# Sine product of the indexer queries behind the first head's shift, query root ahead of the keys' squares, value transposition one chunk later

## The reference

```python
(fq, fk, fv, ff, dq, dk, dv, iq, ik, iw, mq, g) = jnp.split(u @ w_in[l], SPLIT_POINTS, axis=-1)
fq = rmsnorm(fq.reshape(B, S, FOX_HEADS, FOX_HEAD_DIM), fox_q_norm[l])
fk = rmsnorm(fk.reshape(B, S, FOX_HEADS, FOX_HEAD_DIM), fox_k_norm[l])
o_a = fox_attention(fq, fk, fv, logf)
...
iq = rope(iq.reshape(B, S, IDX_HEADS, IDX_DIM), cos_i, sin_i)
...
km, vm = jnp.split(rmsnorm(mem, mem_norm[l]) @ w_mem_kv[l], 2, axis=-1)
km = rmsnorm(km.reshape(B, M, MEM_HEADS, MEM_HEAD_DIM), mem_k_norm[l])
mq = rmsnorm(mq.reshape(B, S, MEM_HEADS, MEM_HEAD_DIM), mem_q_norm[l])
o_c = memory_attention(mq, km, vm)
```

## Time and profile before

| | us |
|---|---|
| three runs, median | 2227.75 |
| lowest and highest of them | 2225.24, 2231.1 |
| the profiled execution | 2225.2 |
| its span | 2223.1 |
| TensorE busy | 2016.6 (91% of the span) |
| VectorE, GpSimd, ScalarE busy | 1099.5, 1223.2, 505.8 |
| mean granted TensorE clock | 0.962 |

### The profile page before, as it was taken

The page is one execution under the profiler, slowest core; times in us unless marked ns, Lnnn a source line. Parts: engine busy times, 40 slices in busy tenths (PEclk is TensorE's granted clock), DMA queues, the critical chain, the costliest instruction groups (busy, mean ns, idle before and its releaser), DMA issues.

```text
span 2223.1 us, 25286 instructions
## 1 busy us (share of the span) xinstructions
PE 2016.6 (91%) x8955; PEld 1627.6 (73%) x8955; DVE 1099.5 (49%) x1308; ACT 505.8 (23%) x916; POOL 1223.2 (55%) x752
## 2 busy tenths in 40 slices
PE   7999999788877789988999999998898869999996
PEld 6888887467656677777778888885677648888884
DVE  5333520556555558765664333009878685333104
ACT  3111100333333333243121111002266421111001
POOL 4666666245534445634666666654454456666661
PEclk9999999899999999999999999999999979999998
DMA  4333323212211113201233333233200012333220
GB/s 146 95 94 97 101 95 85 69 57 72 62 39 38 39 49 84 86 11 38 87 94 95 97 101 95 95 94 85 67 1 1 20 57 86 100 97 94 95 94 38
DMA packets 259808, 163.83 MB, mean 74 GB/s; under 512 B 30380, under 2 KB 249582, under 8 KB 259614
## 3 DMA queue, kind: packets, MB, share of 16 engines
q1 hardware_dynamic: 258080, 157.90, 24.2%
q10 hardware_dynamic: 1662, 5.06, 0.7%
HBM read 160.81 MB, written 2.13 MB: 73 GB/s over the span
## 4 chain that ended last, share of the span: by engine, by line
PE 74%; DVE 17%; ACT 4%; issue 3%; POOL 2%; ACTq 0%; DMA 0%; POOLq 0%; DVEq 0%; SPq 0%
PE bank L710 12%; PE bank L711 12%; PE bank L712 12%; PE bank L779 5%; PE bank L777 5%; PE bank L778 5%; PE bank L971 3%; DVE work L1910 3%; PE bank L973 3%; PE bank L972 3%; DVE work L1971 2%; PE bank L841 2%; PE bank L1176 1%; PE bank L1177 1%; PE bank L1178 1%
## 5 line engine op out<-in xcount | busy, mean ns | idle before, releaser
L597 POOL TENSOR_TENSOR w_lo<-raw,w_hi 128x1024 fp32r<-128x1024 f32 x298 | 744.5, 2498 | 24.9
L595 POOL TENSOR_SCALAR w_hi<-raw 128x1024 fp32r<-128x1024 f32 x298 | 319.4, 1072 | 735.3 <-PE bank L712 344.4
L710 PE MATMUL bank<-u_hi,w_hi 128*128 128x512 f32 x1184 | 476.7, 403 | 27.9 <-DVE u_lo L1859 18.4
L711 PE MATMUL bank<-u_lo,w_hi 128*128 128x512 f32 x1184 | 465.5, 393 | 0.0
L712 PE MATMUL bank<-u_hi,w_lo 128*128 128x512 f32 x1184 | 465.2, 393 | 0.0
L710 PEld LDWEIGHTS bank<-u_hi,w_hi 128*128 128x128 f32 x1184 | 224.7, 190 | 90.7 <-issue 25.5
L711 PEld LDWEIGHTS bank<-u_lo,w_hi 128*128 128x128 f32 x1184 | 225.3, 190 | 49.7 <-issue 4.8
L712 PEld LDWEIGHTS bank<-u_hi,w_lo 128*128 128x128 f32 x1184 | 225.0, 190 | 47.9
L777 PE MATMUL bank<-hid_hi,w_hi 128*128 (+1 forms) x480 | 186.7, 389 | 0.0
L778 PE MATMUL bank<-hid_lo,w_hi 128*128 (+1 forms) x480 | 186.7, 389 | 0.0
L779 PE MATMUL bank<-hid_hi,w_lo 128*128 (+1 forms) x480 | 186.7, 389 | 0.0
(11 more groups left out here) (462 smaller groups left out, 3304.2 us busy)
## 6 DMA issues: line engine op xcount, KB each, us to landing
raw<-in_w_in SPq DMA_DIRECT2D x52, 512.0 KB, 3.7
raw<-in_ffn_w_gate SPq DMA_DIRECT2D x44, 512.0 KB, 3.8
raw<-in_ffn_w_up SPq DMA_DIRECT2D x44, 512.0 KB, 3.7
raw<-in_ffn_w_down SPq DMA_DIRECT2D x44, 512.0 KB, 3.5
raw<-in_w_gate SPq DMA_DIRECT2D x22, 512.0 KB, 3.7
raw<-in_w_up SPq DMA_DIRECT2D x22, 512.0 KB, 3.7
raw<-in_w_down SPq DMA_DIRECT2D x22, 512.0 KB, 3.7
raw<-in_w_branch SPq DMA_DIRECT2D x12, 512.0 KB, 3.4
```

Of the source, the lines that this page charges most:

```text
L595: pool.tensor_scalar(w_hi[:, s, :], raw[:, k, :], 1.0, 1.0, ALU.mult, ALU.mult).then_inc(hi_done, 1)
L597: pool.tensor_tensor(w_lo[:, s, :], raw[:, k, :], w_hi[:, s, :].bitcast(F32), ALU.subtract).then_inc(split_ready, 1)
L710: pe.matmul(outs[:, 0:n], wh, rhs_hi[:, c, :], start=(c == 0), stop=False)
L711: pe.matmul(outs[:, 0:n], wh, rhs_lo[:, c, :], start=False, stop=False)
```

## The change

Four edits, with no operation added or taken away except that a slot's list is written in another order:

- VectorE: the product of bank 1 and the sines moves out of `fox_tasks` into `turn_first`, behind `diagonal` of the first head of a fox step (of the only head, in memory step 3). Cosines and add stay where they were.
- TensorE: the head sum of the query, which overwrites bank 1, waits for that product (`r_sin`) and no longer for the add (`r_out`). ScalarE's `k_square` still waits for `r_out`.
- ScalarE: `stds` is split. The query's root runs ahead of `k_square`, the key's behind it. In the fox steps the four forget loads move from ahead of `k_square` to behind the key's root.
- TensorE: in the memory panels the value transposition moves from chunk 5 to chunk 6.

```diff
                 pe.wait_ge(h_raw, h + 2)
                 for c in chunks(u + 3, K_BANK, *U):
-                    if c == 5:
+                    if c == 6:
                         pe.wait_ge(h_std, h + 2)
                         values(VR_MEM + i, AUX, W[1], MT)
...
                 for c in chunks(u + 1, K_BANK, *U):
                     if c == 3:
-                        pe.wait_ge(r_out, R_IQ + p + 1)
+                        pe.wait_ge(r_sin, R_IQ + p + 1)
                         head_sum(h, AUX, W[0], blk64)
...
-                def stds():
+                def q_std():
                     head_std(h, AUX, W[0], HD)
+
+                def k_std():
                     head_std(h + 1, AUX, W[2], HD)
...
                 if i == 3:
                     forget_sums(0)
+                q_std()
                 k_square()
-                stds()
+                k_std()
                 load_exp()
                 q_high()
...
                 if p < 3:
+                    q_std()
+                    k_square()
+                    k_std()
                     forget_sums(p + 1)
-                    k_square()
-                    stds()
                     load_exp()
                     q_high()
...
+            def turn_first(p):
+
+                dve.wait_ge(h_out, H_FOX + 2 * p)
+                dve.wait_ge(r_rot, R_IQ + p + 1)
+                dve.tensor_tensor(W[2], bank[AUX][:], sin1[:], ALU.mult).then_inc(r_sin, 1)
+
             def fox_tasks(p):
                 h, s, st = H_FOX + 2 * p, S_FOX + 3 * p, (fst, fst2)[p % 2]
                 q = iq[:, p, :]
-                dve.wait_ge(h_out, h)
-                rope(R_IQ + p, q, AUX, cos1[:], sin1[:], W[2], q)
+                dve.tensor_tensor(q, q, cos1[:], ALU.mult).then_inc(r_cos, 1)
+                dve.wait_ge(r_sin, R_IQ + p + 1)
+                dve.wait_ge(r_cos, R_IQ + p + 1)
+                dve.tensor_tensor(q, q, W[2], ALU.add).then_inc(r_out, 1)
...
                 diagonal(i)
+                if i == 3:
+                    turn_first(0)
...
                     diagonal(h)
+                    if h == 2 * p and p < 3:
+                        turn_first(p + 1)
```

More of the change, by code:

```diff
@@ L1558, in other @@
                     raw_copy(u + 3, K_BANK, iq[:, i, :])
-                return q_square, k_square, stds, q_high, v_copy, k_high, v_high, other
+                return q_square, q_std, k_square, k_std, q_high, v_copy, k_high, v_high, other
             def fox_tasks(p):
@@ L1614, in mem_slot @@
                 tasks = mem_tasks(i + 1) if i < 3 else fox_tasks(0)
-                q_square, k_square, stds, q_high, v_copy, k_high, v_high, other = tasks
+                q_square, q_std, k_square, k_std, q_high, v_copy, k_high, v_high, other = tasks
                 q_square()
@@ L1638, in fox_slot @@
                 if p < 3:
-                    q_square, k_square, stds, q_high, v_copy, k_high, v_high, other = fox_tasks(p + 1)
+                    q_square, q_std, k_square, k_std, q_high, v_copy, k_high, v_high, other = fox_tasks(p + 1)
                 exps(*steps[0])
@@ L1674, in mem_and_fox @@
             def mem_and_fox():
-                q_square, k_square, stds, q_high, v_copy, k_high, v_high, other = mem_tasks(0)
+                q_square, q_std, k_square, k_std, q_high, v_copy, k_high, v_high, other = mem_tasks(0)
                 act.wait_ge(c_stored, 32)
                 q_square()
+                q_std()
                 k_square()
-                stds()
+                k_std()
                 load_exp()
```

## The result

The changed kernel takes 2175.96 us (median of four runs, 2173.9 to 2177.97) against 2227.72 us before (four runs, 2225.24 to 2231.1): a ratio of 0.9767, 95% interval 0.975 to 0.9784. That is 51.8 us faster; the forecast was 47.3 us faster, 2180, and 2170 to 2196 as its range. The profiled execution took 2175.67 us, its span 2173.6 us, so the two profiled executions differ by 49.5.

The account below looks back on a forecast made before the run. TensorE, three quarters of the last chain, was taken to bound the kernel through its waits and half clock. Fox 32.5 plus memory 14.8 make 47.3 us: 2227.75 - 47.3 = 2180, range 2170 to 2196.

Parts of the forecast that it names:

- The waits for the add and the roots (26.3 + 3.6): Fox steps: TensorE's waits for the `iq` add (26.3 us) and for the query root (3.6 us) would go.
- The walk of fox step 1: Fox step 1 followed operation by operation: key's square at 678.65 instead of 688.09, 11.35 us gained in the step.
- The product ahead: Fox steps: the sine product ahead of the second head's maxima delays TensorE's next score by 0.68 us, 2.0 in three.
- The three waits for exponentials: Fox steps: each wait for exponentials shrinks from 2.08 to 1.75 us; together they give back 1.3 us.
- Fox step 0: First fox step: cosines collide with GpSimd's split, the add ends later, and a new 4.2 us wait precedes the key sum.
- The wait goes whole, and with it the half clock behind it: Fox steps: TensorE's wait for the `iq` add vanishes, and the half clock after it too, 7.5 us of clock.
- its bounds: Possible deviations from the forecast, among them half clock behind fox step 0's 4.2 us wait, -2 to -5 us.
- Memory steps: Memory steps: transposition waits (7.0 us) and first step's half clock (3.4) go; last step gives 4.4; together 14.8 us.
- Rival b: Memory steps: the query's low part meets GpSimd's second split pass instead of preceding it; 8 us less gain, 2188; chance 0.12.
- Rival c: Fox steps: remaining waits bring back half clock, costing 5 us each, 15 in three; 2195; chance 0.12.
- Granted clock 1.0 from 475 to 750 us: Expected sign in the trace: TensorE at full clock through the memory and fox steps; its failure would mean Rival c.
- Rivals d and e: Fox steps. d: square keeps its distance behind the add, 2211, chance 0.04. e: forget loads come late, 2235, chance 0.01.

Follow-up runs that it names:

- wait-for-the-add run: Changed kernel with the query's head sum in the fox steps waiting for the add (`r_out`) again, sine product still ahead: 2209.49 us.
- copy of 512 columns: Changed kernel with an added 128x512 ScalarE copy ahead of `q_high` in the four memory steps: 15.8 us slower than the changed kernel.
- The best version: Changed kernel with the sine product in its own buffer and forget loads behind the sixth pair of exponentials: 2169.09 us; again, 2172.08 beside 2177.14.

## Why the prediction was right, point by point

- **The waits for the add and the roots (26.3 + 3.6).** Gone whole, as forecast, and the wait-for-the-add run shows that the wait, not the place of the product, is what cost.
- **The walk of fox step 1.** The key's square was to start right behind the add, and did (kernel after):

```profile
652.35 0.69 DVE L2159 TENSOR_TENSOR iq<-iq,work 128x512 f32<-128x512 f32 x1
```

```profile
653.07 0.60 ACT L1378 ACTIVATE work<-bank 128x512 f32<-128x512 f32 x1 [3.47 <-DVE iq L2159]
```

  What the walk left out is GpSimd: its first pass starts at 652.51, 0.16 us behind the add (0.11 in step 2), so the add of these steps won a race as narrow as that of the memory steps; what losing it costs no run shows. The loads were to cost 0.6 us, and the table load behind them stands 0.65 us late. The wait for the exponential was to be 1.75 and is 1.72. The step gave 10.86 us (53.94 to 43.08) against 11.35, and 12.28 in step 2; the mean is 11.6. The product ahead was to cost 0.68 us and cost 0.60: from second score to head sum are 14.25 us, where 13.65 lay before (without the wait). The three waits for exponentials were to give back 1.3 us, which the forecast's own figure for each, 2.08 to 1.75, doesn't yield (3 x 0.33 = 1.0); they gave 1.7 (6.2 to 4.5). Of the 1.4 us between steps 1 and 2, 1.06 are the half-clock stretch that step 1 has and step 2 hasn't (43.08 against 42.02).
- **Fox step 0.** Forecast 10.66 + 1.21 + 2.3 - 0.68 - 4.2 + 0.3 = 9.6, measured 7.56. The new wait is 4.39 us against 4.2, and the add ended 12.15 us behind the head sum (598.14 to 610.29) against 12.1. How it came there was told slightly wrong: I let the cosines collide with GpSimd's pass and the add follow; the cosines went through and the add collided. What failed is the step "The wait goes whole, and with it the half clock behind it": it held for the long wait, but the new one of 4.39 us has its own stretch, and so has the old one of 1.86, which had none before (1.00 from 601 to 606 us there). The prediction named such a stretch behind the wait of 4.2 us in its bounds, but had it at nothing in its sum, and didn't think of the old wait. Two stretches of 1.0 to 1.2 us each, the price that one had in steps 1 and 2, account for the missing 2.0; neither was priced alone here. The second of them also lies between the head sums of steps 0 and 1, which are 47.55 us apart (598.14 to 645.69) and not 46.
- **Memory steps.** Forecast 7.0 + 3.4 for the first three and the one ahead, measured 10.76 + 1.77 = 12.5; the last one 4.4, measured 4.36. The term was too small by 2.1 us, because an "idle before" is less than what a wait costs. In the third memory step of before:

```profile
557.50 0.39 PE L973 MATMUL bank<-u_hi,w_lo 128*128 128x512 f32 x1
559.81 0.41 PE L817 MATMUL bank<-const,work 128*128 128x128 f32 x2 [1.92 <-ACT work L1310]
...
561.91 0.40 PE L973 MATMUL bank<-u_hi,w_lo 128*128 128x512 f32 x1
562.49 0.36 PE L841 MATMUL bank<-m_kh,m_qh 128*128 128x256 f32 x1 [0.18 <-DVE m_kl L1929]
```

  and of after:

```profile
547.05 0.39 PE L973 MATMUL bank<-u_hi,w_lo 128*128 128x512 f32 x1
547.28 0.38 PE L817 MATMUL bank<-const,work 128*128 128x128 f32 x2
...
548.66 0.39 PE L973 MATMUL bank<-u_hi,w_lo 128*128 128x512 f32 x1
548.89 0.28 PE L841 MATMUL bank<-m_kh,m_qh 128*128 128x256 f32 x1
```

  Records of matmuls overlap: one lasts 0.39 us, but the next starts 0.23 behind it. So the wait of 1.92 us really took 2.31 - 0.23 = 2.08, and the small one of 0.18 in front of the score, which I left out, took 0.58 - 0.23 = 0.35. Together 0.5 us a step above the 1.92; three times that is 1.5 of the missing 2.1.
- **Rival b** did not come, but by 0.26 us. By the forecast's own rows the low part follows the copy by 0.67 us (498.59, 499.26), which puts it at 497.5 to 497.7 and not at 497.4, so 0.2 to 0.4 us ahead of the pass; 0.26 it was. The price, 8 us, was half of what the copy of 512 columns showed.
- **Rival c** came in kind and not in size: waits that were left brought half clock, in stretches that cost 1.0 to 1.2 us each, not 5. The sentence that stood against it, that waits of 2.08 us had full clock behind them, was true of the trace of before and not of the next one. "Granted clock 1.0 from 475 to 750 us" held for the memory steps only; by the prediction's own rule ("if the last one fails, (c)") this would have been rival c, while the time, 2175.96 us, is not its 2195. The sign couldn't tell short stretches from long ones.
- **Rivals d and e.** The square did follow the add, and no first score of a fox step waited for a forget load. The best version issues them later still, and doesn't wait either.
- **The total.** 47.3 forecast, 47.6 by the ledger. The fox steps gave 30.7 against 32.5, the memory steps 16.9 against 14.8: two errors that cancelled. The median moved by 51.8 us, 4.2 more than the stretch gave; 1.9 of these lie outside it in the profiled pair, and the rest is how far one execution stands from the median.

## What to carry to other kernels

Ask of a wait which of the queued operations the waiting engine needs: here one product of 0.68 us freed the bank, and waiting for the add behind it cost 33 us. When a wait goes, look at what shares a scratch tile with it, and at DMA issues that stand in the order of a computing engine; each can be the next wait, and two edits that each remove one may not add because the one moves the other. And price a wait by the distance of the starts on both sides of it, not by the idle time alone.

## What the runs showed of the hardware that I had not expected

- A VectorE operation with two inputs in SBUF (128x512) that starts 0.05 us ahead of GpSimd's second pass takes 0.69 us, one that starts 0.26 us behind it takes 2.69. If VectorE is first, the pass is the longer one: 2.39 us alone, 2.72 with a lead of 0.26, 2.90 with one of 0.05.
- GpSimd's pass seems to be held while its record runs: 3.68 us in fox step 0, with a VectorE product of 0.61 us that went undisturbed inside it, and 2.35 to 2.38 us in the four profiled executions whose product is not there. That the start in a record needn't be the start of the work is inferred from these lengths; why the product was held at the same distance in the last memory step is open.
- Behind a wait of TensorE of 1.7 us the half clock came in six of twelve cases (fox steps 1 and 2, otherwise alike), behind one of 1.1 us in none of eight, and at the same instruction of the same kernel it differed from one execution to the next. A trace of one execution that shows full clock behind a wait doesn't show that it will be so in the next.
